# Expert tiles that move only occupied rows, and results laid out by choice and token

## The reference, cut to what matters

```python
s = sigmoid(t @ w_router)
_, idx = top_k(s + b_router, 4)
sel = take_along_axis(s, idx, -1)
w = sel / sum(sel) * 2.5
gates = einsum("nk,nke->ne", w, one_hot(idx, 32))
hg, hu = einsum("nd,edf->nef", t, w_e_gate), einsum("nd,edf->nef", t, w_e_up)
routed = einsum("nef,efd->nd", silu(hg) * hu * gates[:, :, None], w_e_down)
shared = (silu(t @ w_s_gate) * (t @ w_s_up)) @ w_s_down
x = x + g2 * rmsnorm(routed + shared, g_post2)
```

## Time and profile before

| | |
|---|---|
| Median of 3 runs | 2972.08 us (2966.62 to 2982.61) |
| Profiled execution | 2974.04 us, span 2972.2 us, mean granted clock 0.942 |
| Busy: PE / PEld | 2601.5 us (88%) / 1614.8 us (54%) |
| Busy: DVE / ACT / POOL | 878.8 (30%) / 600.0 (20%) / 244.4 us (8%) |
| DMA | 452.94 MB, 152 GB/s over the span |
| By queue | q1 306.49 MB, q10 82.02 MB, q0 62.92 MB |
| Expert weights loaded | 3 x 78 DMAs of 512 KB |
| Result tiles stored (L2251) | 76 DMAs of 512 KB |
| Filler stores (L1275) | 14 DMAs, 12 of them 2560 KB |

### The profile page before, as it was taken

One profiled execution on the slowest core, in us unless ns is written; L12 is line 12 of the kernel. 1 busy time (PEld: TensorE's weight loads), 2 busy tenths in 40 slices (PEclk: granted clock), 3 DMA queues, 4 the chain that ended last, 5 costly groups with the idle time before them and its releaser, 6 DMA issues. The chain is left out here.

```text
span 2972.2 us, 32531 instructions
## 1 busy us (share of the span) xinstructions
PE 2601.5 (88%) x12052; PEld 1614.8 (54%) x12052; DVE 878.8 (30%) x1843; ACT 600.0 (20%) x1362; POOL 244.4 (8%) x274
## 2 busy tenths in 40 slices
PE   4999969879999989999939998986999999999993
PEld 2445634455447545677615565544545754577771
DVE  1414301451005124322264242136101513422226
ACT  2221100340014012122132121025001401212221
POOL 0005100000000000111220150000000000011113
PEclk8999989989999999999969999989999999899997
DMA  8441086100542030799853101710033203089995
GB/s 305 142 142 36 29 312 244 36 1 29 178 148 51 29 110 36 276 377 379 310 198 122 64 29 33 295 64 1 29 106 109 48 29 116 30 325 379 378 351 219
DMA packets 189027, 452.94 MB, mean 152 GB/s; under 512 B 30732, under 2 KB 52340, under 8 KB 188916
## 3 DMA queue, kind: packets, MB, share of 16 engines
q1 hardware_dynamic: 139668, 306.49, 28.9%
q10 hardware_dynamic: 31968, 82.02, 7.4%
q0 software_dynamic: 17280, 62.92, 5.8%
HBM read 362.00 MB, written 89.39 MB: 152 GB/s over the span
## 5 line engine op out<-in xcount | busy, mean ns | idle before, releaser
L221 PE MATMUL ps<-hT,ring 128*128 128x512 f32 x1408 | 638.1, 607 | 13.2 <-PEq L2632 12.0
L221 PEld LDWEIGHTS ps<-hT,ring 128*128 128x128 f32 x1408 | 267.4, 195 | 339.3 <-issue 339.0
L2138 PEld LDWEIGHTS ps<-mixT,ring 128*128 128x128 f32 x2496 | 284.5, 192 | 96.6 <-issue 96.6
L2138 PE MATMUL ps<-mixT,ring 128*128 128x128 f32 x2496 | 297.1, 277 | 35.5 <-PE ps L2154 33.7
L230 PE MATMUL ps<-ring,hT 128*128 128x512 f32 x480 | 212.5, 601 | 6.8 <-PEq L1168 5.8
L223 PEld LDWEIGHTS ps<-hT,ring 128*128 128x128 f32 x1408 | 171.0, 192 | 42.1 <-issue 42.1
L1993 POOL COPY ex_index<-token_of_slot 128x1 uint32 (+1 forms) x80 | 14.7, 183 | 2102.7 <-DVE token_of_slot L2386 1721.8
L221 PE MATMUL ps<-late,ring 128*128 128x512 f32 x384 | 175.5, 600 | 8.6 <-PEq L1577 2.8
L223 PE MATMUL ps<-hT,ring 128*128 128x128 f32 x1408 | 171.4, 275 | 0.0
L2024 PE MATMUL ps<-ring,mixT 128*128 128x512 f32 x320 | 144.1, 611 | 15.3 <-PEq L2632 15.3
L230 PEld LDWEIGHTS ps<-ring,hT 128*128 128x128 f32 x480 | 91.5, 193 | 120.2 <-issue 118.1
(11 more groups left out here) (377 smaller groups left out, 3040.8 us busy)
## 6 DMA issues: line engine op xcount, KB each, us to landing
ring<-in_w_e_gate SPq DMA_DIRECT2D x78, 512.0 KB, 5.4
ring<-in_w_e_up SPq DMA_DIRECT2D x78, 512.0 KB, 6.5
ring<-in_w_e_down SPq DMA_DIRECT2D x78, 512.0 KB, 8.4
y_rows<-out_gpost ACTq DMA_DIRECT2D x76, 512.0 KB, 6.3
ring<-in_w_in SPq DMA_DIRECT2D x18, 2048.0 KB, 8.7
y_rows<-hT SPq DMA_DIRECT2D x12, 2560.0 KB, 31.3
ring<-in_w_gate SPq DMA_DIRECT2D x12, 2048.0 KB, 9.3
mixT<-in_w_ada ACTq DMA_DIRECT2D x8, 2048.0 KB
```

What stands on the lines that cost most here:

```text
L221: pe.matmul(lat, wide[:, k, c], hT[:, k, CTX:TOK], start=(k == 0), stop=(k == kt_n - 1))
L2138: ins = pe.matmul(ps[:, 2 + b, g * P:(g + 1) * P], ew[:, k, :], xT[:, b, k, :], start=(k == 0), stop=(k == KT - 1))
```

## The change

The table now holds, instead of the token, the row number k x 640 + token + 1 of each place, so that an empty place (0) can be told from token 0. From it VectorE derives two index tables: the token (for gathers) and the row k x 640 + token (for stores); empty places get an index of 4095 or more, which is out of bounds. Gathers and stores carry a bounds check, by which such rows are skipped. The store of a tile's result becomes an indirect scatter issued by GpSimd, after the gather of the tile two further on, and waits for both halves of the evicted result. Two scatters of two rows into spare rows stand at the start of the loop. `y_rows` is laid out by choice and token, so the combination reads contiguous blocks by plain loads on SyncE's queue, eight of them in front of the gate loads and four more per tile later. The filler stores and `slot_of` are gone.

```diff
@@ constants @@
+NO_ROW = 4096.0
-    iota = np.concatenate([np.broadcast_to(b, (P, P)), a + P * np.arange(TILES), a], axis=1).astype(np.float32)
+    iota = np.concatenate([np.broadcast_to(b, (P, P)), a + P * np.arange(N_CHOICE) + 1, a], axis=1).astype(np.float32)
@@ stage_da, SyncE @@
-            spare = UNROLL * (MAX_TURNS - MIN_TURNS)
-            for a in range(0, spare, TILES):
-                n = min(TILES, spare - a)
-                sp.dma_start(cx.y_rows[UNROLL * MIN_TURNS + a:UNROLL * MIN_TURNS + a + n].rearrange("t p d -> p t d"),
-                             cx.hT[:, :, :].rearrange("p k n -> p (k n)")[:, 0:n * D].rearrange(
-                                 "p (t d) -> p t d", d=D)).then_inc(sem("rows_filled"), 16)
             load_behind(cx, sp, L, ("in", "dq"), ("in", "dv"))
@@ stage_tail, POOL @@
                 pool.indirect_dma_start(xg[:, b, :], None, cx.h_rows,
-                                        bass.IndirectOffsetOnAxis(ap=index[:, b:b + 1], axis=0)).then_inc(
-                    sem(f"xg_ready{b}"), 16)
+                                        bass.IndirectOffsetOnAxis(ap=index[:, b:b + 1], axis=0), bounds_check=TOK - 1,
+                                        oob_is_err=False).then_inc(sem(f"xg_ready{b}"), 16)
+
+            def scatter(n, i):
+
+                b = n % 2
+                pool.wait_ge(sem("y_low"), at(n + 3, i))
+                pool.wait_ge(sem("y_high"), at(n + 3, i))
+                pool.tensor_copy(goal[:, b:b + 1], m.dest[:, bass.ds(at(n, i), 1)]).then_inc(sem("goal_ready"), 1)
+                pool.wait_ge(sem("goal_ready"), at(n + 1, i))
+                pool.sem_inc(sem("pool_go"), 1)
+                pool.indirect_dma_start(cx.y_rows, bass.IndirectOffsetOnAxis(ap=goal[:, b:b + 1], axis=0), y[:, b, :],
+                                        None, bounds_check=TOP_K * TOK - 1, oob_is_err=False).then_inc(
+                    sem(f"y_stored{b}"), 16)
...
             pool.wait_ge(sem("table_known"), 1)
+            for b in range(2):
+
+                pool.indirect_dma_start(cx.y_rows, bass.IndirectOffsetOnAxis(ap=goal[0:2, b:b + 1], axis=0), y[0:2, b, :],
+                                        None).then_inc(sem(f"y_stored{b}"), 16)
             pool.wait_ge(sem("rows_stored"), 16 * TILES)
             gather(0)
             gather(1)
             with pool.Fori(0, count) as i:
                 for n in range(2, UNROLL + 2):
                     gather(n, i)
+                    scatter(n - 2, i)
+            for b in range(2):
+                pool.wait_ge(sem(f"y_stored{b}"), count * (16 * UNROLL // 2) + 16)
@@ stage_tail, ScalarE @@
                     silu_up(n, i)
-                    act.wait_ge(sem("y_low"), at(n + 2, i))
-                    act.wait_ge(sem("y_high"), at(n + 2, i))
-                    act.dma_start(cx.y_rows[bass.ds(at(n - 1, i), 1)].rearrange("o p d -> (o p) d"),
-                                  y[:, b, :]).then_inc(sem(f"y_stored{b}"), 16)
-            for b in range(2):
-                act.wait_ge(sem(f"y_stored{b}"), count * (16 * UNROLL // 2) + 16)
-
-            act.sem_inc(sem("act_go"), 1)
@@ stage_tail, VectorE @@
                     ins = dve.tensor_scalar(where[:, n, :], iota[:, 0:TABLE], chosen[:, k, 1, t:t + 1],
-                                            token[:, t:t + 1], ALU.is_equal, ALU.mult)
+                                            place_of[:, n:n + 1], ALU.is_equal, ALU.mult)
...
-                dve.scalar_tensor_tensor(out=m.slot_of[:, k, :], in0=chosen[:, k, 1, :], scalar=float(P),
-                                         in1=chosen[:, k, 0, :], op0=ALU.mult, op1=ALU.add)
...
             dve.wait_ge(sem("table_mm"), 1)
-            dve.tensor_copy(m.table[:, :], ps[:, 3, 0:TABLE]).then_inc(sem("table_known"), 1)
+            known = ps[:, 3, 0:TABLE]
+            for b in range(2):
+                dve.tensor_scalar(goal[:, b:b + 1], col, float(TOP_K * TOK + 2 * b), None, ALU.add)
+            dve.tensor_scalar(tab[:, 0, :], known, 0.0, NO_ROW, ALU.is_equal, ALU.mult)
+            step(dve, dve.tensor_scalar(tab[:, 2, :], known, float(TOK), None, ALU.is_gt))
+            for k in range(2, TOP_K):
+                step(dve, dve.scalar_tensor_tensor(out=tab[:, 2, :], in0=known, scalar=float(k * TOK), in1=tab[:, 2, :],
+                                                   op0=ALU.is_gt, op1=ALU.add))
+            step(dve, dve.scalar_tensor_tensor(out=tab[:, 1, :], in0=known, scalar=-1.0, in1=tab[:, 0, :], op0=ALU.add,
+                                               op1=ALU.add))
+            dve.scalar_tensor_tensor(out=m.table[:, :], in0=tab[:, 2, :], scalar=-float(TOK), in1=tab[:, 1, :],
+                                     op0=ALU.mult, op1=ALU.add)
+            dve.tensor_copy(m.dest[:, :], tab[:, 1, :]).then_inc(sem("table_known"), 1)
...
-            for b in range(2):
-                dve.sem_inc(sem(f"y_stored{b}"), 16)
@@ stage_combine @@
-        @block.gpsimd
-        def _(pool):
-            for n in range(N_CHOICE):
-                t, k = n // TOP_K, n % TOP_K
-                if n >= BUFS:
-                    pool.wait_ge(sem("yg_used"), n - BUFS + 1)
-                pool.indirect_dma_start(yg[:, n % BUFS, :], None, cx.y_rows.rearrange("n p d -> (n p) d"),
-                                        bass.IndirectOffsetOnAxis(ap=m.slot_of[:, k, t:t + 1], axis=0)).then_inc(
-                    sem(f"yg_ready{n % BUFS}"), 16)
...
         @block.sync
         def _(sp):
+            def load_rows(t):
+
+                for k in range(TOP_K):
+                    n = t * TOP_K + k
+                    if n >= BUFS:
+                        sp.wait_ge(sem("yg_used"), n - BUFS + 1)
+                    sp.dma_start(yg[:, n % BUFS, :], cx.y_rows[k * TOK + t * P:k * TOK + (t + 1) * P, :]).then_inc(
+                        sem(f"yg_ready{n % BUFS}"), 16)
+
+            load_rows(0)
+            load_rows(1)
             load_gate(cx, sp, L, 1, gpost, old[:, 3, :], old[:, 4, :], sem("co_gains"))
             if more:
                 load_mods(cx, sp, L + 1, 0, mods, sem("co_mods_in"))
                 load_section(cx, sp, L + 1, 0)
             for t in range(TILES):
+                if t + 2 < TILES:
+                    load_rows(t + 2)
                 sp.wait_ge(sem("x2_ready"), t + 1)
@@ trunk @@
-    cx.y_rows = nc.dram_tensor("y_rows", [UNROLL * MAX_TURNS, P, D], F32, kind="Internal").ap()
+    cx.y_rows = nc.dram_tensor("y_rows", [TOP_K * TOK + 4, D], F32, kind="Internal").ap()
```

13 lines of the change are left out of this document (6 added, 7 removed).

## The result

The changed kernel takes 2994.93 us (median of 11 runs, 2983.11 to 3016.75); the kernel before, on the same chip in the same session, 2975.43 (11 runs, 2966.62 to 2982.87). The ratio is 1.0062 (95% interval 1.0043 to 1.0081): slower by 0.6%, where 2954 and faster was the forecast. The median lies just inside the stated range of 2942 to 2995, at its far end; the direction was wrong. The profiled execution after took 2990.3 us, with a span of 2988.2, 16.0 more than before.

A forecast was written before the change was run, and what follows sets the result against it. TensorE, busy in 88% of the span, was taken as the bound, so savings count only where it waits. Terms -24.4 + 0 + 1.5 - 2 + 6.9 = -18.0 us took 2974.04 to 2956.0, hence a 2954 median; range 2942 to 2995.

The forecast's parts named there:

- Fillers: Attention stage, layer 0: without filler stores three rounds of ada products take 34.7 us instead of 59.07; 24.4 us gained.
- the zero of layer 1: Attention stage, layer 1: removing the filler stores gains nothing, since TensorE covers them.
- Loop traffic: Expert loop: gathers and stores shrink to rows in use, but TensorE doesn't wait for them; 0, at most 4 us gained.
- faster still: Rival, expert loop: less DMA traffic shrinks the gap before the up product or TensorE's work; 15 us, time 2939; chance 0.06.
- Order on POOL: Expert loop: scatters precede gathers on POOL's queue, leaving 7.1 us for a landing of 6.4 or less; 0 lost.
- the first rival: Expert loop: POOL's chain of scatter, gather and landing becomes the bound; 50 us lost, time 3004; chance 0.16.
- the gather lands no sooner: Expert loop: partition sets the DMA engine, so skipped rows unload only half the engines; landing stays at the old median.
- Before the loop: Loop start: extra VectorE instructions and two small scatters delay the first gather by 4.0 us; 1.5 us lost over both layers.
- End of the loop: Loop end: the last scatter lands before TensorE and VectorE's end matters; 1 us gained a layer, 2 in all.
- Combination: Combination: eight row loads queue ahead of gate loads; 5.9 us lost in layer 1, 1 in layer 0, 6.9 together.
- given back in part: Rival: the loop waits now and then, 7 to 22 us, or the combination loses its 16; time about 2968; chance 0.18.

The follow-up runs named there:

- b1: Kernel before, with layer 0's filler stores issued behind the attention stage's output stores; 2958.8 us, ratio 0.991.
- a8: Changed kernel with the seven filler stores back at their old place in both layers, into their own scratch; 3020.13 us, ratio 1.013.
- b3: Kernel before, with layer 0's filler stores behind the attention stage's output stores and layer 1's left out; 2952.69 us, ratio 0.9915.
- a3: Changed kernel with GpSimd issuing the gather of tile n+3 ahead of the scatter of tile n; 2981.9 us, ratio 1.0012.
- a7: Changed kernel with a small ScalarE copy behind a wait for each gather's landing, to date it; 3001.35 us, one run.
- a4: Changed kernel with gathers of all 128 rows without bounds check, and a ScalarE copy dating each landing; 2991.91 us, one run.
- a1: Changed kernel with small marker copies on GpSimd and ScalarE behind the expert loop and its final waits; 2987.75 us, one run.
- a10: Changed kernel with gate loads first, gathers ahead of scatters, and the final waits for scatters and gathers moved to ScalarE; 2963.34 us, ratio 0.9948.
- b4: Kernel before, with GpSimd also waiting for the landing of the last result stores, then making one copy; 2997.2 us, ratio 1.0059.
- a2: Changed kernel with the combination's gate loads issued ahead of the row loads; 2984.9 us, ratio 1.0018.
- a5: Changed kernel with gate loads ahead of row loads and each gather ahead of the scatter of two tiles earlier; 2965.66 us, ratio 0.9966.
- b8: Kernel before, with GpSimd waiting for the last result stores, then a 128-row scatter, its landing and one copy; 3009.33 us, one run.
- b6: Kernel before, with GpSimd waiting for the last result stores, then making eight small copies; 3000.44 us, one run.

## Why the prediction was wrong

The forecast for the profiled execution was 18.0 us gained, and 16.0 were lost. The largest single term was right. Four others missed on the same side, the order on POOL by 10.8 us, the end of the loop by 10.1, the combination by 4.1 and the start of the loop by 3.6; another 5.8 were in no term.

1. *Fillers, -24.4.* Right: of the table's -26.6, 1.8 lie ahead of the stage, which leaves -24.8; the waits are gone as told, and b1, a8 and b3 confirm place, size and the zero of layer 1. The three rounds that were priced saved 24.1 us (34.95 from 59.07); the wait in front of them, left out of the sum, saved another 1.4, and later rounds lost 0.8. b1 says more: the gain never needed the change.

2. *Loop traffic, 0.* Right. The DMA share fell to 0.88 and TensorE gained nothing by it, as a3 shows. The gap in front of the up product stayed (0.39 to 0.49 us), so the rival "faster still" fell.

3. *Order on POOL, 0 "with half a microsecond to spare".* Wrong, and this is the step that the prediction itself marked as thin. The chain to the gather's issue was 7.0 us, not 6.7: the scatter's issue takes 1.03 us, not 0.97, and each copy with its gap 1.06, not 0.97. So 6.9 us were left, not 7.1, and the landing has its median at 6.6 (a7) and its most at 8.6, where the sum took "the median or less" for every round. A median below the limit does not make the cost zero when the landings scatter around it: about 8.2 us went in the ten waits that are not the first, and 10.8 us over both loops (3.6, and 9.8 less 2.6 for the slow first up product). The mechanism is that of the first rival, but its price of 50 us needed issues of 1.94 us, and none was above 1.07.
   What skipping does can be read in the packets. The software queue had 17280 = 120 x 128 x 9/8 before; after, the same rule with 80 gathers and 76 scatters of 128 gives 22464 of the 22592. So a skipped row still sends a packet, but a tiny one: in the kept trace the queue has 10,248 packets of 4096 bytes and 12,344 of 4 bytes, with medians of 159 and 9 ns. The Trainium skill, "DMA: Bandwidth & Descriptors", section "The descriptor swizzle", has 8 data descriptors and one for completion per engine, for a plain transfer of 1 MiB to 128 partitions, which is this 9/8. At 9 ns the tiny packets hardly hold a landing up. The section's rule that the partition sets the engine, quoted in the prediction for "the gather lands no sooner", agrees with a7 and a4; no run here shows which engine took which packet, so why the landing stays is not shown.

4. *Before the loop, +1.5.* 5.1: the wait for the first gather rose by 2.5 in layer 1, at the far end of "0 to 2.4" (the gather landed 6.8 us after its issue, not 4.0 to 6.4), and 2.6 came from a term that was not in the sum: TensorE stood for 3.15 us, and its granted clock fell to 0.50 for the next up product.

5. *End of the loop, -2.* Wrong in sign: +8.1. The prediction asked when the scatter lands, and was on the safe side there (4.0 us taken, 2.3 to 3.3 measured). It did not ask what the engine that issues it does afterwards. Before, GpSimd's last gather came 15 us ahead of the block's start, and its DRAIN was over 7 us ahead of it; a1, a10 and b4 show that GpSimd needs 3.6 us and more even in the kernel before once it comes last, and 6.6 to 7.4 here. The change did two things at once: it made GpSimd the last one out, and by the 38 and 42 scatters more in each block it made the DRAIN 3.1 and 3.4 us longer.

6. *Combination, +6.9.* 11.4 up to the first sum, of which 0.4 came back. The mechanism held, as a2 shows by undoing it. The size was off: the bytes were divided by 381 GB/s, but 6.3 MB in 19.4 us is 325 GB/s, and the eight row loads take SyncE 4.03 us to issue before the first gate load can start.

7. *Not in the sum.* 5.8 us: the two stretches with unchanged work lost 7.7, and 1.8 were gained ahead of the attention stage, where nothing changed either. In the first stretch the two timelines can be laid over each other matmul by matmul. They run apart by 3.0 us from 542 to 552 (times of the kernel after) and by another 1.2, back and forth, from 610 to 633; elsewhere they keep their distance. In the first place the granted clock is 0.50 after and 1.00 before:

```profile
540.60:550.80 10.20, 8.62 (x30) 5.30 (x31) 4.89 (x10) 3.81 (x10) 0.00 (x0) 0.50 0.01 2
...
566.40:576.70 10.30, 6.68 (x43) 4.55 (x45) 7.57 (x16) 5.74 (x15) 0.00 (x0) 1.00 0.01 2
```

   That looks like variation from one execution to the next. Ahead of the loop of layer 0, from 500 to 1230 us, TensorE spent 96 us at the lower clock in this trace and 82 in the one before; but a3 and a5, which hold the change, have 82 too, and over all kept traces the figure runs from 72 (b8) to 106 (b6), both made from the kernel before. Why b4's four runs all have 0.932 to 0.935, and lose 11 us more than its own place shows, stays open.

In sum: -24.8 + 5.1 + 10.8 + 8.1 + 11.0 + 5.8 = 16.0. Of the forecast cases "given back in part" was the nearest in kind. The two places that it names, waits in the loop and the combination, took 14.9 us more than the sum had, and its price was 14. What it lacked, some 19 us, lay at the two ends of the loop and in the clock.

## What to carry to other kernels

A part of a change that gains should be tried alone: moving the fillers gave 0.991 with nothing else (b1), the whole change 1.0062, and mended in three places still only 0.9948 (the intervals of the first and the last just touch). When a queue's work moves to another engine, price all of that engine's time: its issues in the chain of each round, and its DRAIN at the block's end, which only shows when it becomes the last. Compare a limit with the spread of what must fit into it, not with its median. What must land first goes into the queue first: two groups of loads swapped were worth 0.4%.

## What the runs showed of the hardware

- An indirect DMA that skips rows by a bounds check saves their bytes, not their packets (4 bytes and 9 ns instead of 4096 and 159), and its landing hardly changes (median 6.6 us in a7, 6.8 with all rows in a4); its issue takes 1.04 us, not 0.97.
- GpSimd's DRAIN at the end of a block takes 0.082 to 0.084 us for each indirect DMA that it issued in the block, of 2 rows or 128: 1.69 us for 20, 3.16 for 38, 6.27 for 76, 6.92 for 84. When GpSimd comes last, the next block starts 3.4 to 4.0 us after its last instruction in the kernels made from the one before, and 6.6 to 7.4 in those from the changed one. ScalarE, the last one out before, needed 2.97 from its last store's issue, of which 2.8 were the landing (by b4).
- After a wait of 3.15 us at the start of the loop, TensorE's granted clock was 0.50, and its next 32 matmuls took 6.42 us instead of 3.81 (in a3, after 3.04 us, 6.53).
